# A two-layer decoder trunk on one core: where gated products, embedding products, exponentials and a constant product stand

## The chip, the cores and the metric

The kernel runs on one core of one Trainium2 chip (trn2). Its time is the device time in microseconds (us) of one launch. The engines are PE (TensorE, matrix products), DVE (VectorE), ACT (ScalarE), POOL (GpSimd) and SP (SyncE, which issues most DMAs). Each engine runs its own list of instructions in order; semaphores tie the lists together. All data is float32.

## The reference, cut to what matters

Two layers over 256 tokens of width 1024. Layer 0 mixes tokens with a convolution module, layer 1 with sparse attention. Each is followed by a mixture of 32 experts and a gated embedding. The parts that the change touches:

```python
# layer 0, token mixer
u = xn @ w_pw1 + b_pw1                      # 1024 -> 2048
a, g = split(u, 2)
u = a * sigmoid(g)                          # the gated product
u = depthwise_conv(u, w_dw, 31 taps, causal) + b_dw
u = silu(layer_norm(u, ln_g, ln_b)) @ w_pw2 + b_pw2

# experts, both layers
lg = xf @ w_rg + b_rg                       # 4 groups
pg = softmax(lg); pg_sel, grp = top_k(pg, 1)
le = xf @ w_re + b_re                       # 32 experts, the 8 of the group
top_v, top_i = top_k(le of grp, 2)
wts = softmax(top_v) * pg_sel
# tokens are sorted by expert; each expert: (silu(x @ w_gate) * (x @ w_up)) @ w_down

# embedding, both layers
h = h + sigmoid(rms_norm(h, g_ple) @ ple_w_gate) * (p[i] @ ple_w_proj)
```

## The kernel before

There is no scheduler: the order of each engine's instructions is the order of the code in that engine's block. Nothing is planned at run time but the number of extra rounds of an expert with over 32 tokens.

**Convolution.** The 1024 channels are worked in 8 chunks of 128 (on the partitions), with the 256 tokens along the row. For a chunk `c`, PE computes both halves of `u` into bank `c % 4` of PSUM; ACT takes the sigmoid of the gate half (L1142); DVE multiplies (`glu(c)`, L1397), which gives `cv0[:, c]`. 15 of the 31 taps are then done on DVE, in two running sums (`cT` in the tensor `hn`, and `accb` in `arena`; L1428, L1430, L1432, closed by L1441). The other 16 taps are done on PE in stacks of four, for which ACT makes 16 shifted copies of the chunk (L1158) and POOL builds diagonal weights (L1027). DVE adds PE's part later (`taps_out`, L1403, two chunks behind). Sums for the layer norm are kept by ACT (squares, L1128) and POOL (L1019, L1021). In chunk 6 POOL also adds the bias of the last projection to `h`, in two instructions (L1036). After the last chunk come the layer norm and the projection `w_pw2` on PE (L565).

`GLU_AHEAD = 4` says where the gated product stands: those of chunks 0 to 3 at the start of their own chunk, those of chunks 4 to 7 in the middle of the taps of the chunk before:

```python
if w == DVE_TAPS // 2 and GLU_AHEAD <= c + 1 < KD:
    glu(c + 1)
```

ACT's loop over chunks is: sigmoid of `c`, squares of `c - 3`, 16 copies of `c` once `glu(c)` is done.

**Routing.** PE computes the 36 router products (L487). DVE picks group and two experts (L1473 to L1523) and so gets `Cc`, a 0/1 table of token by expert (`rt_c`). PE turns it into running counts with a triangular matrix (`upper`, L635) on top of a constant product, expert number by 256 (`iote`, L632): together the prefix product, `rt_pf`. DVE adds the count of each chosen expert to give the slot numbers `S4` (L1534, L1537, `rt_s`). ACT takes two exponentials (L1192, L1194); from these DVE makes the weights `W4`. PE spreads `S4` over rows (L644), gathers the first expert's tokens (L575, `ga_mm`), ACT copies them (`xg`, L1198), PE transposes them (L581), then spreads `W4` (L644 again) and starts the expert loop (gate and up L588, down L603, scatter L610).

**Embedding products.** `p[i] @ ple_w_proj` has four output tiles `(n, t)`, half of the width by half of the tokens, each from two products `c = 0, 1` of 128 rows (L474), and a copy on ACT each (`products`, L1184). They are independent of the routing and stand between its steps on PE and ACT. Their result is read after the experts.

**Loads.** SP issues the weights of the experts into two slots of `ring`, 6 MB an expert. The loads of expert `e + 2` wait until expert `e` has done its gate and up products (L321). Some pieces of later experts are loaded ahead of the loop into other tensors; one of these waits until ACT has copied `h` into PSUM (L346, L347).

## Time and profile before

| | |
|---|---|
| median of 3 runs | 1318.81 us (1316.24 to 1321.77) |
| profiled execution | 1320.43 us, span 1318.5 us |
| mean granted TensorE clock | 0.893 |
| PE, DVE, ACT, POOL busy | 79%, 24%, 23%, 34% of the span |
| convolution's taps on DVE | 23 to 104 us |
| routing of layer 0, from the last router product to the first expert | 148 to 164 us |
| routing of layer 1 | 827 to 842 us |
| mean DMA rate over the span | 341 GB/s |

A row of the profile's order in time says when a group of equal instructions starts and how long it takes, in us, then the engine, the line of the kernel, the operation, what it writes and reads, shapes, and how many; in brackets stands for how long the engine sat idle before and what released it. TensorE runs a float32 product in two records, so `x2` of L474 is one product of 128x512. Durations of neighbouring DVE instructions overlap a little: a tap of 0.47 follows the one before by 0.40.

### The profile page before, as it was taken

What the parts mean: (1) busy time and instruction counts of PE and PEld (TensorE: products, weight loads), DVE (VectorE), ACT (ScalarE), POOL (GpSimd) and SP (SyncE); (2) the same over time, 40 slices, a digit from 0 to 9 for tenths busy, and PEclk for the clock granted to TensorE, in tenths of its full rate; (3) what the DMA queues carried; (4) which work ended last, traced back from release to release, by engine and by line L of the source; (5) the groups of instructions that cost most, each with busy time, mean ns of one, the idle gap of its engine ahead of it and who ended that gap; (6) DMA issues with size and microseconds to landing.
All of it is one profiled execution on the core that took longest, in us unless ns stands there. A gap on an engine that the chain in (4) does not pass through costs nothing.

```text
span 1318.5 us, 26879 instructions
## 1 busy us (share of the span) xinstructions
PE 1041.9 (79%) x10408; PEld 590.8 (45%) x10409; DVE 321.5 (24%) x890; ACT 300.5 (23%) x708; POOL 451.9 (34%) x743
## 2 busy tenths in 40 slices
PE   6968977776688777769998789886777688678778
PEld 5744544333345443334454554443333355344433
DVE  3795300000022000004126681310000121001112
ACT  4873221111111111112212581211111111112111
POOL 2240064334445434340000130354333455434420
PEclk9988889888888888889999699988888898889989
DMA  9942499999999999999424604699999999999990
GB/s 300 392 167 75 160 360 430 429 427 428 428 429 417 429 429 427 427 429 383 157 64 151 296 2 182 280 382 429 428 429 429 428 428 425 428 428 429 429 403 32
DMA packets 63728, 449.28 MB, mean 341 GB/s; under 512 B 11441, under 2 KB 22313, under 8 KB 38856
## 3 DMA queue, kind: packets, MB, share of 16 engines
q1 hardware_dynamic: 58064, 448.25, 82.2%
q10 hardware_dynamic: 5624, 0.51, 0.3%
q8 instruction: 23, 0.38, 0.1%
q14 instruction: 17, 0.14, 0.0%
HBM read 447.70 MB, written 1.05 MB: 340 GB/s over the span
## 4 chain that ended last, share of the span: by engine, by line
DMA 42%; PE 41%; DVE 9%; issue 3%; ACT 3%; SPq 1%; POOL 0%; ACTq 0%; DVEq 0%
DMA ring<-in_moe_w_up 41%; PE PS L588 16%; PE PS L462 9%; PE PS L565 2%; PE PS L603 2%; ACT arena L1158 1%; PE PS L610 1%; PE PS L474 1%; PE PS L575 1%; DVE hn L1432 1%; DVE arena L1432 1%; PE PS L754 1%; PE PS L450 1%; SPq L321 1%; DVE ppw L1788 1%
## 5 line engine op out<-in xcount | busy, mean ns | idle before, releaser
L588 PE MATMUL PS<-ring,arena 128*32 128x256 f32 x4160 | 340.7, 493 | 176.3 <-DMA ring<-in_moe_w_up 157.6
L588 PEld LDWEIGHTS PS<-ring,arena 128*32 128x32 f32 x4160 | 163.6, 136 | 345.3 <-issue 209.9
L1486 DVE TENSOR_TENSOR arena<-PS,arena 64x256 f32<-64x256 f32 x65 | 27.8, 428 | 580.2 <-ACT arena L1223 574.4
L603 PE MATMUL PS<-ring,arena 128*32 128x256 f32 x2080 | 125.7, 381 | 30.8 <-DVE arena L1489 30.8
L1223 ACT ACTIVATE arena<-PS 64x256 f32<-64x256 f32 x64 | 24.2, 378 | 521.1 <-PE PS L588 521.1
L991 POOL TENSOR_SCALAR arena<-arena 128x32 f32<-128x32 f32 x64 | 18.9, 295 | 285.4 <-PE PS L575 282.8
L950 POOL TENSOR_SCALAR arena<-arena 128x512 f32<-128x512 f32 x67 | 105.7, 1578 | 27.1 <-ACT arena L1200 14.2
L603 PEld LDWEIGHTS PS<-ring,arena 128*32 128x32 f32 x2080 | 73.1, 109 | 61.1 <-issue 37.3
L944 POOL TENSOR_SCALAR arena<-arena 128x32 f32<-128x32 f32 x260 | 88.7, 364 | 13.1 <-POOL arena L991 12.9
L952 POOL TENSOR_TENSOR arena<-arena 128x512 f32<-128x512 f32 x67 | 85.5, 1276 | 5.6
L610 PE MATMUL PS<-arena 32*128 32x256 f32 x1040 | 74.5, 397 | 6.6 <-ACT arena L1221 0.6
L575 PE MATMUL PS<-hn,arena 128*32 128x256 f32 x1072 | 76.8, 397 | 1.6 <-issue 1.6
L1481 DVE TENSOR_TENSOR arena<-PS,g 128x256 f32<-128x256 f32 x67 | 28.5, 425 | 173.8 <-PE PS L581 173.8
L462 PE MATMUL PS<-wb,xnT 128*128 128x512 f32 x160 | 70.0, 593 | 0.6 <-DVE xnT L1370 0.6
L997 POOL TENSOR_SCALAR arena<-arena 128x1 f32<-128x1 f32 x64 | 23.0, 359 | 135.5 <-PE PS L610 135.4
L1227 ACT COPY arena<-PS 128x256 f32<-128x256 f32 x64 | 23.9, 374 | 162.6 <-PE PS L603 162.6
L610 PEld LDWEIGHTS PS<-arena 32*128 32x128 f32 x1040 | 50.3, 183 | 17.4 <-issue 17.4
L939 POOL TENSOR_TENSOR rstd<-rstd,nhalf 128x1 f32<-128x1 f32 x12 | 7.1, 595 | 138.4 <-DVE rstd L1362 138.4
L954 POOL TENSOR_TENSOR arena<-arena 128x256 f32<-128x256 f32 x67 | 49.0, 731 | 5.3
L575 PEld LDWEIGHTS PS<-hn,arena 128*32 128x32 f32 x1072 | 36.6, 110 | 27.2 <-issue 3.1
L1223 ACT ACT_TABLE_LOAD x32 | 41.1, 1283 | 24.8 <-issue 24.8
L462 PEld LDWEIGHTS PS<-wb,xnT 128*128 128x128 f32 x160 | 30.0, 190 | 36.8 <-issue 36.8
(328 smaller groups left out, 1211.6 us busy)
## 6 DMA issues: line engine op xcount, KB each, us to landing
ring<-in_moe_w_up SPq DMA_DIRECT2D x62, 2048.0 KB, 22.4
ring<-in_moe_w_down SPq DMA_DIRECT2D x62, 2048.0 KB, 24.1
ring<-in_moe_w_gate SPq DMA_DIRECT2D x60, 2048.0 KB, 18.0
wb<-in_ple_w_gate SPq DMA_DIRECT2D x4, 2048.0 KB, 32.3
ring<-in_conv_w_pw SPq DMA_DIRECT2D x3, 2048.0 KB, 18.9
ring<-in_nsa_w_in SPq DMA_DIRECT2D x3, 2048.0 KB, 17.5
wb<-in_moe_w_gate SPq DMA_DIRECT2D x2, 2048.0 KB, 14.5
wb<-in_moe_w_up SPq DMA_DIRECT2D x2, 2048.0 KB, 10.5
```

The lines of the kernel that those rows point to most:

```text
L462: i = pe.matmul(PS[:, bank, :], lhs[:, k, t * P:(t + 1) * P], w[:, k, :], start=start and k == 0, stop=(k == KD - 1))
L575: i = pe.matmul(PS[32 * j:32 * j + 32, BGX, 0:Q4].rearrange("q (p c) -> q p c", c=2), lhs[:, t, :], rows[:, j], start=(t == 0), stop=(t == ...
L588: i = pe.matmul(PS[32 * j:32 * j + 32, BGU, 0:256].rearrange("q (p c) -> q p c", c=2), xT[:, k, :], w[:, k, :].rearrange("q (p h c) -> q h ...
L603: i = pe.matmul(PS[32 * j:32 * j + 32, BY, 0:Q4], hT[:, c, 32 * f:32 * f + 32], w_dn(s)[:, f, c, Q4 * j:Q4 * (j + 1)], start=(q == 0), sto ...
L610: i = pe.matmul(PS[:, ACC + j, 256 * t:256 * (t + 1)], w[32 * j:32 * j + 32, t * P:(t + 1) * P], ysb[32 * j:32 * j + 32, :], start=False, ...
L944: i = g.tensor_scalar(eq4[:, t, k, :], c32, S4[:, t, k:k + 1], None, ALU.is_equal)
L950: g.tensor_scalar(eqr, srow, cc, None, ALU.is_equal).then_inc(count, 1)
L952: g.tensor_tensor(eqr, eqr, wrow, ALU.mult).then_inc(count, 1)
L954: g.tensor_tensor(to, eqr[:, 0, :], eqr[:, 1, :], ALU.add).then_inc(ok, 1)
L1223: nc.scalar.activation(gs[64:128, :], PS[0:64, BGU, 0:256], ACT.Silu).then_inc(sil_ok, 1)
L1481: return v.tensor_tensor(dst.rearrange("p (j c) s -> p j c s", c=2), PS[:, BGX, Q4:Q4 + 256].rearrange("p (c j s) -> p j c s", c=2, j=4), ...
L1486: return v.tensor_tensor(hh[64:128, :], PS[64:128, BGU, 0:256], gs[64:128, :], ALU.mult)
```

## The change

There are four edits.

1. `GLU_AHEAD` becomes 7. The gated products of chunks 4, 5 and 6 go from the middle of the chunk before to the start of their own chunk; only that of chunk 7 stays in the middle.
2. On PE, of the last embedding tile (1, 1) the first product goes from ahead of the prefix product to behind it, ahead of the product that spreads `S4`.
3. On PE, the wait for `Cc` goes behind the first constant product.
4. On ACT, the copies of the embedding tiles stand apart: one, the first exponential, two, the second exponential, the copy of the gathered rows, the last.

```diff
-GLU_AHEAD = 4
+GLU_AHEAD = KD - 1
...
                 for n, t in ((0, 1), (1, 0)):
                     for c in range(2):
                         embedding_product(L, n, t, c)
-                embedding_product(L, 1, 1, 0)
 
                 pe.wait_ge(const_ok, 2)
-                pe.wait_ge(rt_c, 2 * L + 1)
                 for t in range(NT):
                     pe.matmul(PS[:, 6, 32 * t:32 * t + 32], ones[0:1, :], iote[0:1, :], start=True, stop=False)
+                    if t == 0:
+                        pe.wait_ge(rt_c, 2 * L + 1)
...
                 g0 = (NE + 1) * L
+                embedding_product(L, 1, 1, 0)
                 pe.wait_ge(xt_act, 2 * a + 2)
                 pe.wait_ge(rt_s, 2 * L + 2)
                 rows(S4, 6).then_inc(rt_row, 1)
...
-                def products(n):
-                    for t in range(NT):
-                        act.wait_ge(pp_mm, 4 * L + 2 * n + t + 1)
-                        nc.scalar.copy(pp[:, t, 512 * n:512 * (n + 1)], PS[:, 2 * n + t, :]).then_inc(pp_ok, 1)
+                def product(n, t):
+                    act.wait_ge(pp_mm, 4 * L + 2 * n + t + 1)
+                    nc.scalar.copy(pp[:, t, 512 * n:512 * (n + 1)], PS[:, 2 * n + t, :]).then_inc(pp_ok, 1)
...
-                products(0)
+                product(0, 0)
                 act.wait_ge(rt_d, 2 * L + 1)
                 nc.scalar.activation(eg, dg, ACT.Exp).then_inc(rt_e, 1)
+                product(0, 1)
+                product(1, 0)
                 act.wait_ge(rt_d, 2 * L + 2)
                 nc.scalar.activation(sm[:, 4, :], sm[:, 3, :], ACT.Exp).then_inc(rt_e, 1)
-                products(1)
                 g0 = (NE + 1) * L
                 act.wait_ge(ga_mm, g0 + 1)
                 nc.scalar.copy(xg, PS[:, BGX, 0:Q4]).then_inc(xg_ok, 1)
+                product(1, 1)
```

On DVE, chunk 3 from its taps in the middle to the start of chunk 4. Before, L1397 is the gated product of chunk 4, L1441 closes chunk 3, L1403 adds PE's taps of chunk 2:

```order
L1432 SCALAR_TENSOR_TENSOR arena<-ppw,arena 128x256
L1397 SCALAR_TENSOR_TENSOR ppw<-PS,vecT,arena 128x256
L1432 SCALAR_TENSOR_TENSOR hn<-ppw,arena,hn 128x256
L1432 SCALAR_TENSOR_TENSOR arena<-ppw,arena 128x256
...
L1441 TENSOR_TENSOR hn<-hn,arena 128x256
L1403 TENSOR_TENSOR hn<-PS,hn 128x256
```

After (the lines of these are two further down, L1399, L1443, L1405 and L1434):

```order
L1434 SCALAR_TENSOR_TENSOR arena<-ppw,arena 128x256
L1434 SCALAR_TENSOR_TENSOR hn<-ppw,arena,hn 128x256
L1434 SCALAR_TENSOR_TENSOR arena<-ppw,arena 128x256
...
L1443 TENSOR_TENSOR hn<-hn,arena 128x256
L1399 SCALAR_TENSOR_TENSOR ppw<-PS,vecT,arena 128x256
L1405 TENSOR_TENSOR hn<-PS,hn 128x256
```

The gated product of chunk 4 moved behind seven taps and the closing sum of chunk 3.

On PE, the routing of layer 0 from the router products to the gather. Before:

```order
L487 MATMUL PS<-wr,xnT 128x36 x16
L474 MATMUL PS<-ppw,arena 128x512 x6
L632 MATMUL PS<-iote,ones 128x32
L635 MATMUL PS<-arena,upper 128x32
L632 MATMUL PS<-iote,ones 128x32
L634 MATMUL PS<-arena,ones 128x32
L635 MATMUL PS<-arena,upper 128x32
L638 MATMUL PS<-ones,arena 32x1 x2
L644 MATMUL PS<-ident,arena 128x128 x4
L575 MATMUL PS<-hn,arena 32x256 x4
```

After:

```order
L487 MATMUL PS<-wr,xnT 128x36 x16
L474 MATMUL PS<-ppw,arena 128x512 x5
L630 MATMUL PS<-iote,ones 128x32
L635 MATMUL PS<-arena,upper 128x32
L630 MATMUL PS<-iote,ones 128x32
L634 MATMUL PS<-arena,ones 128x32
L635 MATMUL PS<-arena,upper 128x32
L638 MATMUL PS<-ones,arena 32x1 x2
L474 MATMUL PS<-ppw,arena 128x512
L644 MATMUL PS<-ident,arena 128x128 x4
L575 MATMUL PS<-hn,arena 32x256 x4
```

One embedding product of six moved from ahead of the prefix product to behind it.

On ACT, the same place, from the scaling of `h` to the copies into PSUM. Before, L1192 and L1194 are the exponentials and L1198 the copy of the gathered rows:

```order
L1088 ACTIVATE hn<-h,rstd 128x1024
L1184 COPY ppw<-PS 128x512 x2
L1192 ACT_TABLE_LOAD
L1192 ACTIVATE arena<-arena 128x8
L1194 ACTIVATE arena<-arena 128x2
L1184 COPY ppw<-PS 128x512 x2
L1198 COPY arena<-PS 128x256
L1200 COPY arena<-PS 128x512
```

After:

```order
L1089 ACTIVATE hn<-h,rstd 128x1024
L1184 COPY ppw<-PS 128x512
L1192 ACT_TABLE_LOAD
L1192 ACTIVATE arena<-arena 128x8
L1184 COPY ppw<-PS 128x512 x2
L1196 ACTIVATE arena<-arena 128x2
L1199 COPY arena<-PS 128x256
L1184 COPY ppw<-PS 128x512
L1202 COPY arena<-PS 128x512
```

Of the four copies one moved behind the first exponential with its table, one ahead of the second exponential, and one behind the copy of the gathered rows.

## Rows read from the trace of the kernel before

**Rows 1.** the page's chain that ended last, shares of the span by engine.

```profile
DMA 42%; PE 41%; DVE 9%; issue 3%; ACT 3%; SPq 1%; POOL 0%; ACTq 0%; DVEq 0%
```

**Rows 2.** stretches: start:end, length, busy of each engine, PE clock, DMA share, GB/s.

```profile
160.00:164.00 4.00, 2.98 (x20) 1.52 (x14) 1.43 (x6) 0.90 (x3) 0.00 (x0) 1.00 0.02 4
836.00:840.00 4.00, 3.78 (x23) 1.09 (x22) 0.81 (x5) 0.18 (x1) 0.00 (x0) 0.64 0.01 6
```

**Rows 3.** SP queue in order of time: start, length, what.

```profile
168.47 0.35 SPq L321 DMA_DIRECT2D ring<-in_moe_w_gate  x1
```

**Rows 4.** VectorE, convolution, in order of time: start, length, line, instruction, idle before.

```profile
60.84 0.48 DVE L1397 SCALAR_TENSOR_TENSOR ppw<-PS,vecT,arena 128x256 f32<-128x256 f32 x1 [4.28 <-ACT arena L1142]
...
66.58 1.27 DVE L1432 SCALAR_TENSOR_TENSOR hn<-ppw,arena,hn 128x256 f32<-128x256 f32 x1
...
79.20 0.47 DVE L1397 SCALAR_TENSOR_TENSOR ppw<-PS,vecT,arena 128x256 f32<-128x256 f32 x1
...
80.12 2.58 DVE L1432 SCALAR_TENSOR_TENSOR arena<-ppw,arena 128x256 f32<-128x256 f32 x1
...
92.53 0.47 DVE L1397 SCALAR_TENSOR_TENSOR ppw<-PS,vecT,arena 128x256 f32<-128x256 f32 x1
...
96.33 0.42 DVE L1403 TENSOR_TENSOR hn<-PS,hn 128x256 f32<-128x256 f32 x1
...
104.11 0.76 DVE L1403 TENSOR_TENSOR hn<-PS,hn 128x256 f32<-128x256 f32 x2
```

**Rows 5.** ScalarE, convolution, same columns.

```profile
61.42 6.77 ACT L1158 COPY ppw<-ppw 32x268 f32<-32x268 f32 x16 [0.37 <-DVE ppw L1397]
...
86.56 0.47 ACT L1142 ACTIVATE arena<-PS,vecT 128x256 f32<-128x256 f32 x1
...
93.09 6.77 ACT L1158 COPY arena<-ppw 32x268 f32<-32x268 f32 x16 [4.08 <-DVE ppw L1397]
```

**Rows 6.** PE, convolution's last taps and the projection behind it.

```profile
100.00 3.64 PE L513 MATMUL PS<-arena 128*32 128x256 f32 x32 [8.08 <-ACT arena L1158]
...
110.51 15.67 PE L565 MATMUL PS<-ring,xnT 128*128 128x512 f32 x32 [3.37 <-ACT xnT L1171]
```

**Rows 7.** POOL, convolution, chunk 6.

```profile
79.20 0.72 POOL L1021 TENSOR_TENSOR arena<-arena 128x256 f32<-128x256 f32 x1 [1.79 <-ACT arena L1128]
79.88 5.04 POOL L1036 TENSOR_TENSOR h<-h,wb 128x1024 f32<-128x1024 f32 x2
```

**Rows 8.** PE, routing of layer 0 up to the second expert.

```profile
147.57 8.00 PE L474 MATMUL PS<-ppw,arena 128*128 128x512 f32 x12
...
158.00 1.13 PE L644 MATMUL PS<-ident,arena 128*128 128x128 f32 x8 [0.65 <-DVE arena L1537]
...
160.45 1.13 PE L474 MATMUL PS<-ppw,arena 128*128 128x512 f32 x2
162.53 0.51 PE L581 MATMUL PS<-ident,arena 128*128 128x128 f32 x2 [0.95 <-ACT arena L1198]
...
179.65 5.68 PE L588 MATMUL PS<-ring,arena 128*32 128x256 f32 x64 [5.88 <-issue]
```

**Rows 9.** ScalarE, routing of layer 0.

```profile
155.05 0.19 ACT L1194 ACTIVATE arena<-arena 128x2 f32<-128x2 f32 x1
...
161.62 0.59 ACT L1184 COPY ppw<-PS 128x512 f32<-128x512 f32 x1 [5.91 <-PE PS L474]
162.10 0.38 ACT L1198 COPY arena<-PS 128x256 f32<-128x256 f32 x1
```

**Rows 10.** VectorE, routing of layer 0.

```profile
152.73 0.23 DVE L1523 TENSOR_TENSOR arena<-arena 128x64 f32<-128x64 f32 x1
...
157.18 0.36 DVE L1534 TENSOR_TENSOR arena<-PS,arena 128x64 f32<-128x64 f32 x2 [0.95 <-PE PS L635]
```

**Rows 11.** VectorE, routing of layer 1.

```profile
831.95 0.23 DVE L1523 TENSOR_TENSOR arena<-arena 128x64 f32<-128x64 f32 x1
```

**Rows 12.** PE, routing of layer 1.

```profile
840.73 0.51 PE L581 MATMUL PS<-ident,arena 128*128 128x128 f32 x2 [0.95 <-ACT arena L1198]
```

## The prediction

> **What bounds the kernel now.** I read the chain of waits first: DMA has 42% of it and PE 41% [rows 1]. The two expert stages run at the pace of their weight loads, and nothing in the change touches their bytes or their order; they can only start sooner. So the question is which stretches stand ahead of them. The table by stretches answers it: from 160 to 164 us the DMA share is 0.02 [rows 2], and the SP queue issues the next expert's loads at 168.47, right after the first expert's gate and up products on PE, which release it [rows 3]. DMA is idle while the routing of layer 0 is worked out, so each us saved in the convolution or in the routing should start this stream a us sooner. The same holds for layer 1, where 836 to 840 moves nothing.
>
> The sum is made against the profiled execution: 1320.43 us, of which 1318.5 is the span. The median of the runs shown is 1318.81, 1.6 lower; I subtract the same difference from it.
>
> **Convolution, gated products at the chunk's start (chunks 4 to 6).** No instruction is added or removed; three VectorE instructions of 0.47 us move. The VectorE rows [rows 4] show the cost of the old place: in chunk 3 it stands idle 4.28 us in the middle of its taps (until 60.84), because ScalarE's sigmoid of chunk 4 ends only then. ScalarE is behind there with its 16 copies of the chunk before (6.77 us a chunk, [rows 5]). In the new order the seven taps left run inside that idle time. Worked through:
>
> One measure serves for all: chunk 7, from adding chunk 5's taps to the end, takes 7.78 (96.33 to 104.11, [rows 4]). Two of its taps were held by POOL, about 0.47 each, so it is 6.84 free. Its seven last taps and the closing sum are 3.40 (92.53 to 96.33 is 3.80, with a product of 0.40 in it). The longer POOL instruction of each chunk, the builder of the tap weights, holds a tap for 1.27 instead of 0.47 (66.58, [rows 4]), so 0.8.
>
> Chunk 3: VectorE stopped at 56.5 (60.84 less 4.28). Seven taps and the sum, 3.40, and two of POOL's instructions that fell into the idle time and now beside the taps, 0.8 and 0.47: end 61.15. The sigmoid released the product at 60.84, so the gated product of chunk 4 runs at 61.15, 0.3 later than before.
>
> Chunk 4: 61.15 + 0.40 product + 6.84 + 0.46 for one addition more than in chunk 7 + 1.75 held = 70.6. ScalarE's copies of chunk 5 then start within 0.1 of where they did.
>
> Chunk 5: 70.6 + 0.40 + 6.84 + 1.3 held = 79.1. There stands the product of chunk 6, before at 79.20 [rows 4]. So up to here ScalarE gains nothing, while VectorE is a half chunk and a stall further.
>
> Chunk 6: POOL's bias adds (79.88, 5.04 for two, [rows 7]) now fall into its first taps, each holding one tap as at 80.12 (2.58 instead of 0.47, [rows 4]); with the builder behind them 5.0. First half of the chunk 6.84 - 3.40 = 3.44, product 0.40 at its head, POOL's two small instructions 0.95: 79.1 + 9.8 = 88.9. There stands the product of chunk 7, the only one left in the middle; its sigmoid ended at 87.03 [rows 5] and does so still. Before it ran at 92.53. **Gain 3.7.**
>
> From here both chains move by it: ScalarE's last 16 copies start at 89.4 instead of 93.09 (it sat idle 4.08 before them, [rows 5]), PE's last taps, which waited 8.08 for them, at 96.3 instead of 100.00 [rows 6], and VectorE's own end at 100.4 instead of 104.11. I take 3.7; bounds 4.3 (the whole idle time) and 0 (ScalarE's copies of chunk 6 slide until they eat all that VectorE gains).
>
> Here a rule bears on it. The row: the gated product of chunk 6 ran beside POOL's add of 79.20 [rows 7] in its plain 0.47 [rows 4], while the tap of 80.12 was held. The Trainium skill (SBUF — State Buffer, "Who interferes with whom") says that a VectorE instruction with at most one SBUF input, outside the two-port modes, never contends with GpSimd, and that one with two inputs does. This product reads PSUM and one arena tensor, so by the rule it passes the adds even when it is late. Were it held like a tap, the sum would lose up to 1.5 whenever it comes after 79.88.
>
> **Routing, layer 0, prefix product.** PE's six embedding products end at 155.57, though the choice counts they hide were ready at 152.96 [rows 8, 10]. One product (1,1,0) goes behind the prefix: two of the 12 records of that row. Twelve take 8.00, two alone 1.13 with the end counted [rows 8]; the last three products, which run after the clock came back, take 0.86 each. The small products of the prefix end 0.86 sooner, so their sum can be used at 156.3. VectorE stood 0.95 idle until 157.18 for it [rows 10]. It can't take all: the weights it computes first wait for the second exponential. This now stands behind two copies on ScalarE; the second can begin when product (1,0) ends, 155.57 - 0.86 = 154.7; with 0.48 for the copy the exponential starts at 155.2 instead of 155.05 [rows 9]. The table load and first exponential moved ahead, into time in which ScalarE waited for PE. VectorE then is at the prefix at 156.45, 0.7 sooner. PE runs the displaced product meanwhile, 156.5 to 157.4, and then the row product that stood at 158.00: gain 0.6. If the low clock of the first products lasted over all six, two of them in front of copy (1,0) would take 1.71 instead of 0.86, the exponential would be 1.7 later and this term -1; the upper bound is the 0.95 of idle time.
>
> **Routing, copy of the gathered rows.** Before, ScalarE copied the last embedding product first (161.62) and the gathered rows at 162.10, though the gather ended before the last product began at 160.45; PE sat 0.95 us idle before its transposes at 162.53 [rows 8, 9]. Now the copy of the gathered rows falls beside PE's last embedding product (160.45, 1.13) and the transposes follow that product at once: gain 0.95. The last embedding copy then lies under the transposes and the second row product; its reader comes after them. Bounds 0.5 to 0.95. Layer 0 together 1.55.
>
> **Routing, layer 1.** Here the counts come at 832.18 [rows 11], after the products, so taking one away frees nothing: only the constant product ahead of the wait saves its 0.33, and the displaced product eats nearly all of it before the row product. Gain 0.1. The copy gives its 0.95 again (the idle time before 840.73, [rows 12]). Together 1.05; bounds 0.5 and 2.4, the latter if the clock, 0.64 in 836 to 840 [rows 2], holds at full.
>
> **Sum**: 3.7 + 1.55 + 1.05 = 6.3. 1320.43 becomes 1314.1, and the median 1318.81 becomes **1312.5**. What is late next in both layers is the first expert's gate and up product, and then the load stream.
>
> **Rivals.**
> 1. The bias adds cut in earlier: the sum that closes chunk 5 slips 0.8 us past 79.88 and is held by the first add (2.5). Then the product of chunk 6 runs at 82.3, ScalarE's copies end at 89.7, and the last gated product waits for its sigmoid till 90.3: convolution 2.2 instead of 3.7, time 1314.0. For it: my count over 20 us has a slack of 0.8; against it: ScalarE, which releases the adds, moves with it.
> 2. The stream doesn't start sooner. PE idles 5.88 us before the second expert's products (179.65, [rows 8]) without a named cause; if that ends at a fixed time, or the loads have slack to take, little is left: 1316 to 1319. Against it: loads of the next expert wait by name on PE [rows 3], and DMA is idle before.
> 3. Clock, the good way: layer 1's stretch at a grant of 0.64 [rows 2], 3.8 us of work there, runs at 2.4 GHz and saves 1.4: 1311.1. For it: PE has less idle time there. Against: the stretch ahead is as thin as before.
> 4. Slower: TensorE falls to 1.2 GHz over the projection behind the convolution. Its first 16 products took 15.67 [rows 6]; at the 0.86 of a product at 2.4 GHz they would take 13.8, so 1.9 is lost there already. For it: PE has a long pause (8.08) before the last taps. If half clock lasted over the first 24 products they would lose 20.6, 18.7 more than now: net 12.4 slower, 1331.2. It decides from eight products more at half clock than before (8 x 0.86 = 6.9 against my 6.3), and at sixteen it is slower by over 0.5%. Against it: the pause and what follows are the same in length, 3.7 us sooner.
>
> **Chances.** Forecast 0.58, rival 1 0.12, rival 2 0.14, rival 3 0.10, rival 4 0.05, 0.01 for what I don't see, on the slow side. Of change and no change a measurement tells apart about 0.5%, 6.6 us, so the line lies at 1312.2, just below my forecast, whose own range is 1311.3 to 1314. Faster by over 0.5%: a little under half of the forecast (0.27) and rival 3, 0.37. Slower: rival 4 and the rest, 0.06. Within 0.5%: 0.57. The range leaves out rival 4 and the far end of 3, and holds rival 2: 1309.5 to 1318.8.
>
> **What would show it.** No idle VectorE in chunk 3 and the gated product of chunk 4 near 61.2; of chunk 6 near 79.1; of chunk 7 near 88.9; last taps on PE near 96.3. In the routing VectorE's wait for the prefix gone, transposes with no idle PE before them, SP's issue of 168.47 near 163.2. Wrong if the gated product of chunk 7 still runs after 91, if the exponential is later than VectorE's other work by over 0.5, or if SP's issue moves and the end does not.

## The result, and the profile after

The changed kernel took 1309.10 us (median of 4 runs, 1307.34 to 1311.23), the kernel before 1320.29 beside it on the same chip (4 runs, 1316.24 to 1322.53): ratio 0.9918, 95% interval 0.9894 to 0.9942. It is 11 us faster, 0.8%. The forecast was 1312.5, with a range of 1309.5 to 1318.8: the sign was right, the gain too small, and the time lies 0.4 below the range. The profiled execution took 1310.65 with a span of 1308.7, against 1320.43 and 1318.5, so 9.8 us of the gain can be followed in the two traces.

The chain that ended last (against [rows 1]) has lost PE's share and gained DMA's, as it should when what stands ahead of the load streams gets shorter. The load queue's issue that stood at 168.47 [rows 3] is at 160.40:

```profile
DMA 44%; PE 39%; DVE 9%; issue 3%; ACT 3%; SPq 1%; POOL 1%; ACTq 0%; DVEq 0%
```

```profile
160.40 0.35 SPq L321 DMA_DIRECT2D ring<-in_moe_w_gate  x1
```

The convolution. VectorE and ScalarE, in order of time (start, length, line, instruction, idle before); the first three groups answer to [rows 4], [rows 5] and [rows 7], the last to [rows 6]:

```profile
58.29 1.08 DVE L1443 TENSOR_TENSOR hn<-hn,arena 128x256 f32<-128x256 f32 x1
59.71 0.48 DVE L1399 SCALAR_TENSOR_TENSOR ppw<-PS,vecT,arena 128x256 f32<-128x256 f32 x1 [0.34 <-ACT arena L1143]
...
76.36 0.48 DVE L1399 SCALAR_TENSOR_TENSOR ppw<-PS,vecT,arena 128x256 f32<-128x256 f32 x1
...
77.67 2.57 DVE L1434 SCALAR_TENSOR_TENSOR arena<-ppw,arena 128x256 f32<-128x256 f32 x1
...
86.45 0.47 DVE L1399 SCALAR_TENSOR_TENSOR ppw<-PS,vecT,arena 128x256 f32<-128x256 f32 x1
...
97.91 0.76 DVE L1405 TENSOR_TENSOR hn<-PS,hn 128x256 f32<-128x256 f32 x2
```

```profile
87.01 6.77 ACT L1159 COPY arena<-ppw 32x268 f32<-32x268 f32 x16 [2.50 <-DVE ppw L1399]
```

```profile
56.15 2.94 POOL L1028 TENSOR_TENSOR ppw<-stk,arena 128x512 f32<-128x512 f32 x1 [6.41 <-PE PS L513]
...
65.12 2.76 POOL L1028 TENSOR_TENSOR arena<-stk,arena 128x512 f32<-128x512 f32 x1 [4.40 <-PE PS L513]
...
77.56 4.91 POOL L1037 TENSOR_TENSOR h<-h,wb 128x1024 f32<-128x1024 f32 x2
```

```profile
93.92 3.64 PE L513 MATMUL PS<-arena 128*32 128x256 f32 x32 [8.14 <-ACT arena L1159]
```

The 4.28 us in which VectorE stood in the middle of chunk 3 are gone; what is left is 0.34 at the head of chunk 4. The last gated product runs at 86.45 instead of 92.53, and PE's last taps at 93.92 instead of 100.00. GpSimd's builder of the tap weights (56.15, 65.12) takes 2.94 and 2.76, and the sum that closes the chunk 1.08.

The routing. PE in layer 0, then in layer 1; they answer to [rows 8] and [rows 12], and the stretch to the second row of [rows 2]:

```profile
150.42 1.12 PE L474 MATMUL PS<-ppw,arena 128*128 128x512 f32 x2
151.39 1.05 PE L644 MATMUL PS<-ident,arena 128*128 128x128 f32 x8
...
153.76 1.12 PE L474 MATMUL PS<-ppw,arena 128*128 128x512 f32 x2
154.72 0.39 PE L581 MATMUL PS<-ident,arena 128*128 128x128 f32 x2
```

```profile
828.67 1.05 PE L644 MATMUL PS<-ident,arena 128*128 128x128 f32 x8
829.66 0.67 PE L575 MATMUL PS<-hn,arena 128*32 128x256 f32 x8
...
831.05 1.12 PE L474 MATMUL PS<-ppw,arena 128*128 128x512 f32 x2
832.01 0.39 PE L581 MATMUL PS<-ident,arena 128*128 128x128 f32 x2
```

```profile
830.00:834.00 4.00, 4.00 (x48) 2.36 (x44) 1.51 (x5) 1.62 (x4) 0.00 (x0) 1.00 0.03 10
```

The displaced embedding product stands behind the prefix (L474 ahead of L644), the transposes (L581) follow PE's last embedding product without idle time in both layers, and in layer 1 the granted clock stays at 1.00 where it had been 0.64.

To see where 9.8 us came from, both traces were cut at issues of the load queue, each of which waits for a named end: the first behind the fourth chunk's pointwise product ("start"), the convolution's end, the router's products, the end of the routing, and the end of the experts, and the same again in layer 1. The first column is the time of the first cut, the others are lengths in us from cut to cut, read from the SP queue's rows of each trace:

```
                start  conv.  proj.  routing 0  experts 0  to layer 1  routing 1  experts 1  to output
before          45.93  58.97  42.90      18.89     405.91      254.41      17.87     406.19      50.67
before, again   46.02  58.78  43.17      18.84     405.38      255.03      17.86     406.28      48.23
after           44.81  53.88  43.17      16.91     407.21      255.06      15.00     406.04      49.89
after, again    44.77  54.01  42.89      16.68     407.08      254.81      15.00     406.31      50.02
```

The gain is 1.1 (start) + 5.1 (convolution) - 0.3 + 2.0 (routing 0) - 1.3 (experts 0) - 0.6 + 2.9 (routing 1) + 0.1 + 0.8 = 9.8. Three of these lie where the kernel was edited: 5.1, 2.0 and 2.9.

### The profile page after: what moved, and what is told of

It is laid out like the page before. It is cut to its first block, busy times and chain, and to the rows that moved or that the text cites. A ratio compares the mean times of both kernels' runs of the same rounds, so it can differ in the third digit from the quotient of the medians.

```text
span 1308.7 us, 26877 instructions
## 1 busy us (share of the span) xinstructions
PE 1033.1 (79%) x10408; PEld 586.4 (45%) x10409; DVE 320.4 (24%) x890; ACT 300.9 (23%) x708; POOL 456.2 (35%) x743
## 3 DMA queue, kind: packets, MB, share of 16 engines
HBM read 447.70 MB, written 1.05 MB: 343 GB/s over the span
## 4 chain that ended last, share of the span: by engine, by line
DMA 44%; PE 39%; DVE 9%; issue 3%; ACT 3%; SPq 1%; POOL 1%; ACTq 0%; DVEq 0%
DMA ring<-in_moe_w_up 43%; PE PS L588 16%; PE PS L462 10%; PE PS L565 2%; PE PS L603 2%; ACT arena L1159 1%; PE PS L610 1%; PE PS L575 1%; PE PS L755 1%; PE PS L474 1%; DVE hn L1434 1%; DVE arena L1434 1%; SPq L321 1%; DVE ppw L1790 1%; PE PS L450 1%
```

## The experiments

All are compared with the kernel before on the same chip; the medians of before were 1318.08 in the first batch, 1318.53 in the second and 1318.72 in the third. The table shows all with the lengths as above (the cuts between are left out):

```
kernel          median (runs)   ratio, 95%               start  conv.  routing 0  experts 0  routing 1
before_again    1318.08 (10)    1.0001 0.9977 - 1.0026   46.02  58.78      18.84     405.38      17.86
after_again     1308.89 (6)     0.9917 0.9889 - 0.9945   44.77  54.01      16.68     407.08      15.00
glu_only        1312.68 (12)    0.9956 0.9940 - 0.9973   46.09  53.79      17.90     408.36      18.91
routing_only    1312.07 (8)     0.9951 0.9929 - 0.9972   44.32  58.74      15.01     406.21      15.00
last_copy       1316.58 (12)    0.9983 0.9962 - 1.0005   44.87  58.91      16.65     404.72      18.75
prefix_only     1315.16 (12)    0.9975 0.9958 - 0.9993   44.99  58.92      17.81     408.20      17.12
glu8            1312.14 (10)    0.9949 0.9930 - 0.9967   44.82  56.71      16.48     409.48      16.47
poke            1307.88 (6)     0.9919 0.9889 - 0.9948   45.43  54.90      16.48     407.04      15.02
early7          1308.58 (5)     0.9909 0.9891 - 0.9926   45.34  53.68      16.46     406.80      15.00
delay5          1312.46 (5)     0.9950 0.9936 - 0.9963   44.53  57.63      15.01     405.96      16.74
pad             1319.91 (10)    1.0007 0.9993 - 1.0022   45.06  58.90      18.66     407.76      20.05
```

**The two kernels again.** The kernel before and the kernel after, unchanged, to learn how far a trace repeats itself.

> The kernel before once more, for a second trace and as a measure of noise: ratio 1 within 0.3%. If the start of the convolution varies by chance, the loads issued at 45.93 in the first trace come up to 1.1 earlier here; if POOL's place among the taps is chance, its builder in chunks 3 to 5 lasts more than 1.3 here somewhere.

> The changed kernel once more, for a second trace. If the gain is what the edits make, it is again 9 to 11 us faster, POOL's builder waits 2 to 3 us in chunks 3 to 5, layer 1's routing runs at full clock, and the expert loads of layer 0, 8 us ahead at 400, are 6 ahead at 420. If parts of it are chance, one of these is gone.

Both totals came back, and so did nearly every length, to 0.6 us: also the clock of each layer's routing (17.87 and 17.86, 15.00 and 15.00). Only the way to the output moved, by 2.4. Two pairs are few, but by them a difference of 1 us in a stretch between two programs is hardly the chance of a single run; whether it comes from the edit is another question. The two stretches that the table leaves out say the same: the projection takes 40.60 (poke) to 43.17, and the way to layer 1 250.96 (routing_only) to 255.06, in kernels whose edits touch neither.

One thing did not come back. In chunk 7 GpSimd asks for an addition 0.14 us after VectorE's ninth tap began, in both executions of the kernel before:

```profile
100.37 0.92 POOL L1021 TENSOR_TENSOR arena<-arena 128x256 f32<-128x256 f32 x1 [2.72 <-ACT arena L1128]
```

```profile
100.40 3.29 POOL L1021 TENSOR_TENSOR arena<-arena 128x256 f32<-128x256 f32 x1 [2.72 <-ACT arena L1128]
```

In the first it got in behind that tap and held the next one (0.94 instead of 0.47); in the second it waited until the taps were done. The two executions of the kernel after differ in the same way, the other way round (3.29, then 0.91).

**The halves.** glu_only is the kernel before with one line:

```diff
-GLU_AHEAD = 4
+GLU_AHEAD = KD - 1
```

routing_only is the kernel after with that line put back to 4.

> Only the gated products of chunks 4 to 6 move; the routing is as before. Theory A (my working, with its one wrong size put right): the seven taps of chunk 3 fill the stall, and in addition POOL's builder now holds the closing sum of a chunk (0.65) where it held taps before (about 1.3 to 1.75 a chunk), so the last taps on PE start 5 to 6 us before those of the kernel before and the whole is 5 faster. Rival B: the traces of before and after differ by 1.1 us before anything changed (45.93 against 44.81), so a part is chance, the edit is worth 3.7 as predicted, and the holding of taps falls in either order by chance. Under A builder instructions of chunks 3 to 5 last 2 to 3 us each, under B some last 1.3.

> Only the edits of the routing, gated products where they were. Theory A: they gain 2.1 in layer 0 and 2.9 in layer 1, where TensorE stays at 2.4 GHz over the row products (before: 0.64 granted in 836 to 840), 4 to 5 us in all, less up to 2 that the expert stream of layer 0 gives back in its middle. Rival B: the clock of layer 1 is chance, the gain there is 1.0 as predicted, and the whole is worth 2.5.

0.44% and 0.49% add up to 0.93%, against 0.83% for both together, well within the intervals. The convolution is 5.2 shorter with the line alone (53.79 against 58.97) and stays at 58.74 without it. The second half gives 2.87 in layer 1 and 3.9 in layer 0 (how much of each is the clock is worked out further down). And it starts the convolution 1.6 sooner, in a stretch that it does not touch. Of the two expectations theory A came true for glu_only (5.4 us faster by the medians; the builders of chunks 3 to 5 take 2.93, 2.74 and 1.92; PE's last taps start 4.9 sooner, where 5 to 6 was written). For routing_only A said 4 to 5 us and B 2.5; it is 6.0 by the medians, with an interval from 3.7 to 9.4. Its trace shows more, 1306.99 against 1320.43, but that execution is the fastest of eight, and 3.5 of it come from the way to layer 1 (250.96), where nothing was edited.

**The two edits of the routing apart.** last_copy changes ScalarE's order only:

```diff
-                products(1)
+                product(1, 0)
 ...
                 nc.scalar.copy(xg, PS[:, BGX, 0:Q4]).then_inc(xg_ok, 1)
+                product(1, 1)
```

> The kernel before with one edit alone: ScalarE's copy of the last embedding product (1,1) goes behind its copy of the gathered rows; the embedding products on TensorE, the prefix and the exponentials stay where they were. Theory A (each edit of the routing has its own part, and the clock of layer 1 follows the gap in front of the transposes): the transposes follow the last embedding product without idle time in both layers, 0.95 us each; in layer 1 that closes the gap of 0.95 after which TensorE fell to half clock, so its stretch from the router load to the accumulator load falls from 17.87 to between 15.5 and 16.9; end 1.9 to 3.3 us earlier than before. Rival B (the clock of layer 1 follows the idle time ahead of the counts, which the prefix edits change): the stretch falls by 0.95 only, to 16.9. Rival C on the start: the convolution starts 1.2 to 1.6 us sooner (first loads on SP behind the up products near 44.5 instead of 46.0) although nothing is edited there, as in the kernel with both routing edits; if it stays at 46.0 the prefix edits carry that, not this one.

prefix_only changes TensorE's order only (the embedding product behind the prefix, the constant product ahead of its wait).

> The kernel before with the two edits of TensorE's program alone: the fourth embedding product (1,1,0) behind the prefix, and the constant product of the prefix ahead of its wait. ScalarE's copies and exponentials stay in their old order, so ScalarE's copy of (1,1) still stands ahead of the gathered rows. Theory A (by what was predicted for these edits): layer 0 0.6 us sooner at the gather, and nothing of the 0.95 before the transposes: stretch from router load to accumulator load 18.9 to about 18.3 in layer 0, 17.8 in layer 1, where the clock stays low. Rival B (the clock of layer 1 follows TensorE's idle time ahead of the counts, where the constant product and the displaced product now stand): layer 1 falls to 16 or below while the 0.95 gap in front of the transposes is still there. Rival C: the second exponential waits for the copies as before, nothing is gained in layer 0, 18.9. On the start: the convolution starts near 44.5 if this part of the program carries that shift, 46.0 if the other edit does.

Layer 0 came to 16.65 with the copy alone and to 17.81 with the prefix alone (18.89 before). The idle time before the transposes goes with the copy and with nothing else. PE in layer 1, of last_copy and then of prefix_only:

```profile
832.00 1.82 PE L474 MATMUL PS<-ppw,arena 128*128 128x512 f32 x2
833.66 0.39 PE L581 MATMUL PS<-ident,arena 128*128 128x128 f32 x2
```

```profile
838.30 1.12 PE L474 MATMUL PS<-ppw,arena 128*128 128x512 f32 x2
840.37 0.51 PE L581 MATMUL PS<-ident,arena 128*128 128x128 f32 x2 [0.95 <-ACT arena L1199]
```

Both expectations on the clock of layer 1 fell. In last_copy the stretch got longer, 18.75, although the gap of 0.95 is gone: PE ran its embedding products at half clock and, after a while at full clock, the gather and the last embedding product too. Two stretches of last_copy:

```profile
817.00:823.00 6.00, 6.00 (x14) 3.54 (x15) 3.44 (x18) 0.59 (x1) 0.00 (x0) 0.50 1.00 426
830.00:833.00 3.00, 3.00 (x21) 0.89 (x14) 0.78 (x5) 0.37 (x1) 0.00 (x0) 0.50 0.00 0
```

So the clock of this stretch does not follow that gap. (Prefix_only, at 17.12, lies between its two forecasts, 17.8 and 16.) On the start the rival was right in both: 44.87 and 44.99, whichever half of the routing is changed.

**All gated products at the chunk's start.** The kernel after with GLU_AHEAD = KD.

> The kernel after, with the last gated product too at its chunk's start (GLU_AHEAD = KD), so none stands amid taps. Theory A (ScalarE's 16 copies of the last chunk set the end of the convolution, and VectorE's product releases them): the product of chunk 7 runs near 89.9 instead of 86.45, ScalarE's copies start near 90.4 instead of 87.01, TensorE's last taps near 97.2 instead of 93.92, and the convolution ends 2.7 to 3.3 us later than in the kernel after; total about 3 us slower than after, still 5 faster than before. Rival B (VectorE's own taps set the end, the last chunk ends at 97.11 there): the end moves by under 1.

VectorE, ScalarE and PE of glu8:

```profile
89.89 0.48 DVE L1399 SCALAR_TENSOR_TENSOR ppw<-PS,vecT,arena 128x256 f32<-128x256 f32 x1
```

```profile
90.46 6.77 ACT L1159 COPY arena<-ppw 32x268 f32<-32x268 f32 x16 [5.93 <-DVE ppw L1399]
```

```profile
97.37 3.64 PE L513 MATMUL PS<-arena 128*32 128x256 f32 x32 [11.56 <-ACT arena L1159]
```

Theory A, to 0.2 us: the convolution is 2.8 longer and the kernel 3 slower than the kernel after. The one product left amid the taps is worth that. Layer 1's routing took 16.47 here, with the routing of the kernel after: the clock fell behind the row product, as in the kernel before.

**A small instruction amid the taps.** In the kernel after, chunks 3 to 5:

```diff
+                    if w == 10 and 3 <= c <= 5:
+                        v.tensor_scalar(cv0[:, KD - 1, 0:8], cv0[:, KD - 1, 0:8], 1.0, None, ALU.mult)
```

> The kernel after, with one small VectorE instruction more in chunks 3, 4 and 5: behind the eleventh of the fifteen taps it multiplies eight columns of zeros of the last chunk by one (one input, nothing changes in them). In the kernel after GpSimd's builder of tap weights, asked for in mid chunk, took 2.94, 2.76 and 1.95 us in these chunks, and VectorE's taps ran on unheld till the sum that closes the chunk, which took 1.08 instead of 0.42. Theory A (a run of VectorE instructions with two inputs that follow each other without a gap keeps GpSimd out until it ends or is broken by one with a single input): the extra instruction lets the builder in; in at least two of the three chunks it takes 1.0 to 2.0 us less, a tap of 1.27 stands behind the extra instruction, and the closing sum is 0.42 again. The chunk gets longer by the extra instruction and the held tap, about 0.3 to 0.6 us each, less 0.66 for the sum. Rival B (GpSimd waits for the gap that a wait makes before the closing sum, or the builder is simply longer by chance): durations and held sums stay as in the kernel after. Time within 1 us of after in both.

GpSimd's builder and VectorE in poke:

```profile
56.78 1.37 POOL L1028 TENSOR_TENSOR ppw<-stk,arena 128x512 f32<-128x512 f32 x1 [6.39 <-PE PS L513]
...
65.75 1.50 POOL L1028 TENSOR_TENSOR arena<-stk,arena 128x512 f32<-128x512 f32 x1 [4.39 <-PE PS L513]
...
74.72 1.16 POOL L1028 TENSOR_TENSOR ppw<-stk,arena 128x512 f32<-128x512 f32 x1 [4.41 <-PE PS L513]
```

```profile
56.76 0.48 DVE L1434 SCALAR_TENSOR_TENSOR hn<-ppw,arena,hn 128x256 f32<-128x256 f32 x1
57.16 1.02 DVE L1443 TENSOR_SCALAR ppw<-ppw 128x8 f32<-128x8 f32 x1
58.09 0.47 DVE L1434 SCALAR_TENSOR_TENSOR arena<-ppw,arena 128x256 f32<-128x256 f32 x1
```

In all three chunks the builder got in at the extra instruction and took 1.37, 1.50 and 1.16 instead of 2.94, 2.76 and 1.95. Two details went otherwise than written: the extra instruction itself took 1.02 (for eight columns), not the tap behind it, and the closing sum stayed held at 0.77, now by GpSimd's next addition:

```profile
58.11 2.23 POOL L1020 TENSOR_TENSOR arena<-hn 128x256 f32<-128x256 f32 x1
```

It was asked for beside the first tap behind the small instruction (58.09) and yet waited until the run was over, 2.23 instead of 0.90, in all three chunks. So a request at the head of a run can be kept out too. The convolution was 1.0 longer, the total the same.

**The last product sooner.** In the kernel after:

```diff
-                    if w == DVE_TAPS // 2 and GLU_AHEAD <= c + 1 < KD:
+                    if w == 4 and GLU_AHEAD <= c + 1 < KD:
```

> The kernel after, with the one gated product that is left amid taps (chunk 7's, in chunk 6) behind the fifth tap instead of the eighth. Its sigmoid ended at 84.2, so it should run at 84.3 to 85.2 instead of 86.45, ScalarE's copies start near 84.9 to 85.7 instead of 87.01, and TensorE's last taps end 1.3 to 2.1 earlier than 97.56. Theory A (in the kernel after TensorE's last taps and VectorE's own chain end within 0.5 of each other, VectorE's closing sum at 97.11): the convolution ends 0 to 0.5 earlier, and the time is that of the kernel after. Rival B (TensorE's last taps alone set the end, as the later product of the kernel with GLU_AHEAD = KD, 2.8 later, would also allow): it ends 1.3 to 2.1 earlier.

VectorE and PE of early7:

```profile
84.84 0.48 DVE L1399 SCALAR_TENSOR_TENSOR ppw<-PS,vecT,arena 128x256 f32<-128x256 f32 x1
...
97.78 0.42 DVE L1443 TENSOR_TENSOR hn<-hn,arena 128x256 f32<-128x256 f32 x1
98.23 0.75 DVE L1405 TENSOR_TENSOR hn<-PS,hn 128x256 f32<-128x256 f32 x2
```

```profile
92.33 3.64 PE L513 MATMUL PS<-arena 128*32 128x256 f32 x32 [6.01 <-ACT arena L1159]
```

Theory A: PE's last taps end at 95.97, 2.3 before VectorE's last two additions begin (98.23), where in the kernel after they end at 97.56, 0.35 before 97.91; and the convolution is only 0.2 shorter (53.68 against 53.88). VectorE's own taps bound it now. The median is the lowest but one; the kernel beats the kernel before, and is not to be told from the kernel after (0.9909 against 0.9917, with intervals of 0.0035 and more).

**A delay of known size.** In the kernel after, behind the last chunk's taps:

```diff
+            for _ in range(11):
+                link(v.tensor_scalar(accb, accb, 1.0, None, ALU.mult))
```

> The kernel after, with eleven VectorE multiplications of the 128x256 tap buffer by one behind the last chunk's taps, each waiting for the one before (about 0.45 each, so 5.0 us in all); nothing reads their result. It measures what a us at the end of the convolution is worth at the end of the program. Theory A (the load stream starts later by what the convolution ends later, and hands it on whole): the convolution ends 4.5 to 5.2 later than in the kernel after, the issue of the next expert's loads as much, the end 4.3 to 5.5, near 1313.7. Rival B (the stream has slack and gives part of a head start back, as the 1.3 us between the accumulator load and the end of layer 0's experts in the kernel after suggest): the time is 2.5 to 4 later only, near 1312. Rival C (part of it is hidden, since TensorE's last taps end at about the same time as VectorE's): the convolution itself ends by less than 4.5 later.

```profile
97.78 3.57 DVE L1445 TENSOR_SCALAR arena<-arena 128x256 f32<-128x256 f32 x11
```

The row of delay5 shows that the eleven took 3.57, not the 5.0 that was written; the convolution is 3.7 longer than in the kernel after, so nothing of them is hidden. The kernel is 3.4 to 3.6 slower than the kernel after by the medians (1312.46 against 1309.10 and 1308.89), 4.3 by the ratios. As written, 1312.46 is nearer to B (1312) than to A (1313.7). With the size corrected it is what A says (3.7), and more than B would leave (half to four fifths of it, 1.9 to 3.0). The two intervals (0.9936 to 0.9963, 0.9889 to 0.9945) overlap, though, so delay5 alone does not settle it. Its trace can't: the profiled execution ends with that of the kernel after (1310.49 against 1310.65), because the routing of layer 0 took 1.9 less (15.01), its experts 1.3 less and the way to layer 1 3.2 less (251.87), and the issue of the next expert's loads is only 1.1 later (161.51). But glu_only (convolution 5.2 shorter, time 5.4 less) and glu8 (2.8 longer, 3.0 to 3.3 more) give the same exchange. By all three, what the convolution ends later, the program ends later.

**Nothing changed but the program's length.** The kernel before, with three small VectorE instructions behind all others:

```diff
             moe(1)
+            for _ in range(3):
+                link(v.memset(accb[:, 0:8], 0.0))
```

> The kernel before, with three VectorE instructions more behind everything else in VectorE's program (a memset of 128x8 each, near 1310 us). Nothing ahead of them is changed. Theory A (the length of the first 32 products of the convolution, 8.23 in the kernel before and 7.14 in the kernel after, depends on how the program lies in memory, not on any edit): the first group takes something other than 8.23, and SP's loads behind the up products are issued at least 0.3 away from 46.0. Rival B (it follows from the edits of the routing, in some way that the profile does not show): it stays at 8.2 and 46.0. Total: within 1.5 us of before in both.

PE's first products of the convolution, in before, after and pad:

```profile
14.08 8.23 PE L532 MATMUL PS<-xnT,wb 128*128 128x256 f32 x32
```

```profile
14.04 7.14 PE L532 MATMUL PS<-xnT,wb 128*128 128x256 f32 x32
```

```profile
13.72 7.72 PE L532 MATMUL PS<-xnT,wb 128*128 128x256 f32 x32
```

Theory A in what it forecast: the start moves by 0.9 although everything ahead of 1300 us is as before. That the place of the program in memory does it is not shown; the run shows only that the program as a whole matters. The routing of layer 1 moved too, by 2.2 (20.05), and the experts of layer 0 by 1.9 (407.76). The total is the same (ratio 1.0007), since these moves went both ways.

## Why the prediction was wrong

**Which stretches count, and that the load stream starts sooner: right.** Rival 2 is out. The issue of 168.47 moved by 8.1 and the end by 9.8, and by glu_only, glu8 and delay5 a us at the end of the convolution is a us at the end of the program, as near as the medians tell (5.4 for 5.2, 3.0 to 3.3 for 2.8, 3.4 to 4.3 for 3.7).

**The convolution: the mechanism right, 3.7 forecast and 5.1 measured.** Counted from the first cut of its kernel (45.93, 44.81), the product of chunk 4 ran at 14.90 (forecast 15.22, before 14.91), that of chunk 6 at 31.55 (forecast 33.17), and that of chunk 7 at 41.64 (forecast 42.97, before 46.60). The step that failed is "1.75 held" of chunk 4 (measured: 0.66, in its closing sum): of the 1.6 us at the product of chunk 6, chunk 3 gave 0.3, chunk 4 1.0 (8.49 from product to product, not 9.45) and chunk 5 0.3 (8.16, not 8.5). I had let the builder and GpSimd's two small instructions each hold a tap, as in the kernel before, where the builder's request came in VectorE's idle time or beside the first two-input tap of a chunk (66.25, just ahead of the tap of 66.58, [rows 4]). In the kernel after VectorE is further on when the request comes, in the middle of a run of taps. There the builder waits till the run ends (2.94 and 2.76, of which about 1.05 is work) and costs the closing sum 0.66; the two small ones then fall beside VectorE's PSUM instructions, which took their plain time. Poke shows that the wait hangs on the run, by cutting it in three chunks of three.

The trace of the kernel before had the case already: in chunk 2, whose successor's product stood at its chunk's start even then, GpSimd's builder and VectorE's closing sum read

```profile
48.31 2.59 POOL L1027 TENSOR_TENSOR arena<-stk,arena 128x512 f32<-128x512 f32 x1 [5.64 <-PE PS L513]
```

```profile
50.10 1.08 DVE L1441 TENSOR_TENSOR hn<-hn,arena 128x256 f32<-128x256 f32 x1
```

I took chunk 4 as the measure and overlooked chunk 2. What lets GpSimd in is not settled by the place in the run alone: its addition of 69.07 in the kernel before was asked for beside the sixth tap of a chunk and got in behind that tap (1.02, the tap of 69.44 held), and the addition of chunk 7 did either in one and the same program. Chunk 6 went nearly as forecast (10.09, forecast 9.8), and rival 1, the bias adds earlier by a whole sum, did not happen: they held two taps, 2.57 and 2.59. (88.9 against 92.53 is a gain of 3.6; the working wrote 3.7.)

The Trainium skill (SBUF — State Buffer, "Who interferes with whom") says that issue order decides who blocks. These rows do not bear that out: by the starts in the profile the builder of 56.15 was asked for ahead of four taps (56.52 to 57.71), which all ran in their plain 0.48 before it got in, and the additions of 100.37 and 100.40 came in the same order and ended oppositely. GpSimd's times in a profile are rough, so this is no more than what the starts say.

**The gated product passes GpSimd's work: right.** In no kernel was it held; at 77.65 in glu_only it took 0.48 beside an addition of GpSimd's.

**Routing, layer 0: 1.55 forecast, 2.0 measured.** From the router's products to the row product it was 9.53 instead of 10.20, so the prefix gave 0.67 (forecast 0.6). From there to the transposes it was 3.33 instead of 4.53. Only 0.95 of these 1.20 is idle time in the row; the clock is no part of it, since it was granted in full from 154 on before and from 148 on after. The rest is overlap: a product that another follows at once gives way after 0.96 (153.76 to 154.72), one before a pause is counted with its whole 1.13 (160.45), and the row product behind a pause is 1.13 instead of 1.05. So a gap of 0.95 was worth 1.2. The step that failed is the size of "gain 0.95". What the clock does to this stretch the table shows with one and the same order: 15.01 at full clock throughout (routing_only, delay5), 16.46 to 16.48 where it is halved behind the row product (glu8, poke, early7), 16.68 and 16.91 where it is halved over the embedding products (both executions of the kernel after, as of the kernel before).

**Routing, layer 1: 1.05 forecast, 2.87 measured.** This is rival 3, given 0.10, on top of what was forecast. The step that failed is the clock, which the sum left at the low grant of [rows 2]. The kernel before, behind its row product:

```profile
834.79 1.41 PE L644 MATMUL PS<-ident,arena 128*128 128x128 f32 x8 [0.65 <-DVE arena L1537]
836.13 1.08 PE L575 MATMUL PS<-hn,arena 128*32 128x256 f32 x8
...
838.45 1.34 PE L474 MATMUL PS<-ppw,arena 128*128 128x512 f32 x2
```

against 1.05, 0.67 and 1.12. Glu8 divides the 2.87, for it has the routing of the kernel after and the low clock where the kernel before has it. Stretches of the kernel before, from 835, and of glu8, from 829:

```profile
835.00:839.00 4.00, 4.00 (x29) 1.99 (x29) 1.74 (x11) 0.00 (x0) 0.13 (x1) 0.57 0.07 31
```

```profile
829.00:833.00 4.00, 4.00 (x30) 2.13 (x28) 2.07 (x13) 0.00 (x0) 0.34 (x2) 0.58 0.27 115
```

The stretch takes 17.87 before, 16.47 in glu8 and 15.00 after: 1.40 is the edits (forecast 1.05), 1.47 the clock (rival 3 said 1.4). Whether the edits bring the clock back is not shown. My argument against it, that the stretch ahead is as thin as before, did not carry. For it speaks a count over both layers: the clock stayed full all the way in 7 of the 14 routings with all routing edits, and in none of the 12 others. Against it: in both orders the low clock falls over the embedding products or behind the row product, and glu_only, with the old order, kept full clock behind the row product of layer 1 and lost it over the embedding products:

```profile
817.00:825.00 8.00, 8.00 (x25) 4.90 (x25) 4.47 (x23) 0.79 (x2) 0.00 (x0) 0.57 0.99 420
829.00:833.00 4.00, 3.35 (x36) 1.96 (x35) 2.71 (x15) 0.00 (x0) 0.34 (x2) 1.00 0.00 0
```

Pad, without any edit ahead of it, took 2.2 more than before. What decides the place stays open.

**What no step of the prediction had.** The start, 1.1: the first 32 products took 7.14 instead of 8.23. Last_copy and prefix_only, whose edits run after 140 us, and pad, whose edit runs at the very end, all shift it, so it belongs to how the whole program is built and not to what the edits do. The prediction put this stretch at nothing. Why it moves stays open; no row shows what those products wait for. And the experts of layer 0 are 1.3 longer with the stream ahead. Pad alone moves them by 1.9, and delay5, whose stream starts nearly as early (161.51), has 405.96; so no give-back is shown there.

In sum: 6.3 forecast; 1.4 more in the convolution, 0.4 in layer 0's routing, 0.35 and the clock's 1.5 in layer 1's, 1.1 at the start, 1.3 lost behind: 9.7 of the 9.8, the other stretches nearly cancelling. Of the 1.1 and the 1.5 the edits can claim nothing for certain; that they and the loss of 1.3 left so little over is in part luck. The range was too narrow by this: it had no term for stretches that change when a program is only built otherwise, by pad 1 to 2 us each, and up to 4 in the way to layer 1.

## What to carry to other kernels

Before you move an instruction past a wait on VectorE, ask where GpSimd's requests will then fall: here its builder cut in behind the first two-input tap of a chunk and held the next (1.27), but late in an unbroken run of taps it waited for the end and held only the closing sum, and one small instruction opened the run to it. Do not take the place alone for a rule: other requests did the opposite, and one did either in two executions of one program. Price both. Take as the unit of doubt not how well a run repeats (here 0.6 us a stretch) but how much a stretch moves when three unrelated instructions are added at the end (here 1 to 2 us, and up to 4 between kernels that differ elsewhere). When the clock differs between two kernels, look for a third that has the order of one and the clock of the other. And to learn what a stretch is worth at the end, put a delay of known size into it, and read its size from the trace.

## What the runs showed of the hardware

- A run of VectorE taps that follow each other without a gap kept GpSimd's 128x512 product out for about 1.9 us (2.94 against 1.05 beside idle VectorE) when it was asked for beside the tenth to thirteenth tap: in chunk 2 of all 13 traces, and in chunks 3 to 5 of all 6 traces in which no small instruction and no gated product stands amid them. A multiplication of 128x8 let it in, and took 1.02 itself.
- Whether GpSimd waits for the end of a run is not the same in two executions of one program: its 128x256 addition beside the ninth tap of chunk 7 took 0.92 and 3.29 in the kernel before, 3.29 and 0.91 in the kernel after.
- Eleven dependent in-place multiplications of 128x256 took 3.57 us, 0.32 each; sums of two such tensors take 0.42.
- The granted clock of a thin stretch is the same in two executions of one program (17.87 and 17.86; 15.00 and 15.00) and another in a program that differs only behind it (20.05). At full clock throughout, with the order of the kernel after, the stretch takes 15.00 to 15.02 in both layers; a low clock somewhere in it adds 1.5 to 1.9.
- The length of the convolution's first 32 products behaves alike: 8.23 twice, 7.14 twice, and 7.14 to 7.95 in the others.
